# MoE down weights as four neighbouring rows per partition, gate and up columns dealt two of every four

## The reference

```
D_MODEL = 1024; SEQ = 512; DEPTH = 2; N_EXPERTS = 16; TOP_K = 2; D_EXPERT = D_MODEL // 2
...
    def expert_block(args):
        xblk, e = args
        h = jax.nn.silu(xblk @ w_gate[e]) * (xblk @ w_up[e])
        return h @ w_down[e]
```

## Time and profile before

| | before |
|---|---|
| time, median of 3 runs | 1109.61 us (1108.69 to 1113.83) |
| time of the profiled execution | 1114.09 us |
| its span in the trace | 1112.4 us |
| granted TensorE clock, mean | 0.939 of full speed |
| TensorE matmul busy | 968.1 us (87%) |
| weight issues: gate, up, down | 32 of each, 2048 KB each |
| HBM read, written | 250.33 MB, 53.74 MB |

### The profile page before, as it was taken

One profiled execution on the slowest core, in us unless ns is written; L12 is line 12 of the kernel. 1 busy time (PEld: TensorE's weight loads), 2 busy tenths in 40 slices (PEclk: granted clock), 3 DMA queues, 4 the chain that ended last, 5 costly groups with the idle time before them and its releaser, 6 DMA issues.

```text
span 1112.4 us, 15368 instructions
## 1 busy us (share of the span) xinstructions
PE 968.1 (87%) x5930; PEld 521.7 (47%) x5930; DVE 446.7 (40%) x909; ACT 163.9 (15%) x384; POOL 185.9 (17%) x304
## 2 busy tenths in 40 slices
PE   7999989999996879987669899968997969898994
PEld 4444344567553434543434454534664534454541
DVE  4799953551110111110675556575411212121116
ACT  0000022301110001000222332433010000010100
POOL 1320020213202022200430001011221210303022
PEclk9999989889998999999779999987998989999997
DMA  9994399946999999999730004200699999999953
GB/s 301 383 410 152 86 342 372 405 165 234 384 385 384 422 372 394 392 407 402 246 148 1 1 1 148 79 1 4 255 371 359 387 382 425 379 412 376 410 209 113
DMA packets 74614, 308.69 MB, mean 277 GB/s; under 512 B 9423, under 2 KB 21627, under 8 KB 58010
## 3 DMA queue, kind: packets, MB, share of 16 engines
q1 hardware_dynamic: 35744, 227.43, 53.2%
q10 hardware_dynamic: 28794, 54.03, 13.1%
q0 software_dynamic: 9984, 25.97, 6.7%
HBM read 250.33 MB, written 53.74 MB: 273 GB/s over the span
## 4 chain that ended last, share of the span: by engine, by line
PE 43%; DMA 21%; issue 17%; DVE 13%; POOL 2%; ACT 1%; ACTq 1%; SPq 1%; POOLq 0%; DVEq 0%
PE ps L724 15%; DMA wring<-in_moe_w_up_dram 9%; DVE arena L1067 7%; PE ps L734 7%; PE ps L624 6%; DMA wring<-in_moe_w_gate_dram 5%; PE ps L683 3%; PE ps L744 3%; DMA arena<-xs_dram 2%; PE ps L923 2%; PE ps L754 1%; DMA wring<-in_conv_w_dram 1%; POOL rstd L1841 1%; SPq L438 1%; PE ps L521 1%
## 5 line engine op out<-in xcount | busy, mean ns | idle before, releaser
L724 PE MATMUL ps<-wring,arena 128*64 128x256 f32 x1536 | 186.4, 398 | 23.3 <-DMA wring<-in_moe_w_gate_dram 16.8
L724 PEld LDWEIGHTS ps<-wring,arena 128*64 128x64 f32 x1536 | 114.2, 143 | 90.0 <-DMA wring<-in_moe_w_gate_dram 20.6
L560 PE MATMUL ps<-arena,wring 128*128 128x512 f32 x256 | 110.4, 593 | 1.4 <-DVE arena L1025 1.4
L1271 DVE COPY arena<-ps 128x256 f32<-128x256 f32 x32 | 13.6, 425 | 221.9 <-PE ps L832 211.2
L1067 DVE SCALAR_TENSOR_TENSOR arena<-arena,dwT 128x512 f32<-128x512 f32 x145 | 100.0, 764 | 0.0
L1855 POOL DMA_DIRECT2D arena<-xs_dram x112 | 59.5, 538 | 206.4 <-DVE arena L1250 164.0
L902 PE MATMUL ps<-wring,arena 128*128 128x512 f32 x192 | 86.5, 606 | 3.5 <-ACT arena L1697 3.5
L734 PE MATMUL ps<-wring,arena 128*64 128x512 f32 x384 | 86.5, 592 | 0.6 <-DVE arena L1271 0.6
L560 PEld LDWEIGHTS ps<-arena,wring 128*128 128x128 f32 x256 | 48.5, 190 | 62.1 <-issue 60.3
L724 PE MATMUL ps<-arena 128*64 128x256 f32 x512 | 63.4, 404 | 13.0 <-DMA arena<-in_moe_w_gate_dram 6.9
L1841 POOL TENSOR_TENSOR rstd<-vareps,half 128x1 f32<-128x1 f32 x20 | 24.7, 1235 | 294.9 <-DVE vareps L1084 294.9
(11 more groups left out here) (231 smaller groups left out, 1078.1 us busy)
## 6 DMA issues: line engine op xcount, KB each, us to landing
wring<-in_moe_w_gate_dram SPq DMA_DIRECT2D x24, 2048.0 KB, 23.6
wring<-in_moe_w_up_dram SPq DMA_DIRECT2D x24, 2048.0 KB, 20.0
wring<-in_moe_w_down_dram SPq DMA_DIRECT2D x24, 2048.0 KB, 19.7
xs_dram<-zero ACTq DMA_DIRECT2D x2, 16384.0 KB, 50.5
arena<-in_moe_w_up_dram SPq DMA_DIRECT2D x8, 2048.0 KB, 23.3
arena<-in_moe_w_down_dram SPq DMA_DIRECT2D x8, 2048.0 KB, 25.8
arena<-in_moe_w_gate_dram SPq DMA_DIRECT2D x8, 2048.0 KB, 28.9
xs_dram<-arena ACTq DMA_DIRECT2D x60, 128.0 KB, 8.8
```

Of the source, the lines that this page charges most:

```text
L560: last = pe.matmul(ps[:, 2 * (c % 4) + h, :], w[:, k, h, (c % 2) * P:(c % 2) * P + P], xT[:, k, :], start=(k == 0), stop=(k == KD - 1))
L724: mm = pe.matmul(ps[h * CAP:(h + 1) * CAP, bank, 0:256], act[:, k, :], w[:, k, h * 256:(h + 1) * 256], start=(k == 0), stop=(k == KD - 1))
```

## The change

Down is now loaded as `(p j)`: partition p takes the four neighbouring rows 4p to 4p+3, one run of 16 KB. For the products to come out in that order, the column groups of gate and up are dealt otherwise: group h takes, of every four neighbouring columns, the two at 2h and 2h+1. The 256 columns of one matmul, which were 256 neighbours, are now 128 pairs (8 bytes) with gaps of 8 bytes between them. Where a result stands is as before, so `stage_h`, `down_products` and `quarter_down` keep their code. No instruction is added, removed or moved on any engine; the down load changes its shape (from 128x2x2048 to 128x4096), and the gate and up matmuls the pattern by which they read the weights.

```diff
-        down_src = moe_w_down.rearrange("l e (h p j) n -> p (l e) h (j n)", h=2, p=P)
+        down_src = moe_w_down.rearrange("l e (p j) n -> p (l e) (j n)", p=P)
...
-                    sp.dma_start(slots[r].rearrange("p (h n) -> p h n", h=2), down_src[:, E * l + e, :, :]
-                                 ).then_inc(s_ring[r], 16)
+                    sp.dma_start(slots[r], down_src[:, E * l + e, :]).then_inc(s_ring[r], 16)
...
+            def columns(w, k, h):
+
+                return w[:, k, :].rearrange("p (i j) -> p i j", j=4)[:, :, 2 * h:2 * h + 2]
+
             def half_products(bank, act, w, signal, first=None):
 
                 for k in range(KD):
                     for h in range(2):
                         mm = pe.matmul(ps[h * CAP:(h + 1) * CAP, bank, 0:256], act[:, k, :],
-                                       w[:, k, h * 256:(h + 1) * 256], start=(k == 0), stop=(k == KD - 1))
+                                       columns(w, k, h), start=(k == 0), stop=(k == KD - 1))
...
                         mm = pe.matmul(ps[q * XROWS:(q + 1) * XROWS, bank, 0:256], xgxT[:, k, :],
-                                       gate_up[i][:, k, h * 256:(h + 1) * 256], start=(k == 0), stop=(k == KD - 1))
+                                       columns(gate_up[i], k, h), start=(k == 0), stop=(k == KD - 1))
```

## The result

The changed kernel is slower by 0.7%: 1123.1 us median of 20 runs (1113.5 to 1129.29) against 1115.41 us median of 20 runs of before (1107.56 to 1132.61); ratio 1.0071, 95% interval 1.0048 to 1.0093. The three runs of before that were known at first had a median of 1109.61 us, so the absolute forecast of 1109 us stood on a low draw; what counts is the ratio, and it is about 8 us. The forecast was no measurable change. The 1123.1 us lie inside its range of 1103 to 1133 us, but in the part that was there for rival 1.

A forecast was written before the change was run, and what follows sets the result against it. TensorE and the DMA engines were both taken as nearly full. The profiled 1114.1 us, minus 1 us for transfers, plus 0 for products, gave 1113 us; less 4.5 us to the median, about 1109 us, range 1103 to 1133 us.

The forecast's parts named there:

- rival 1: Gate, up and quarter products: each jump dear, product up to 3.89 us; likely +8 us (+3 to +22), chance 0.18.
- The transfers: Down loads on SP's queue: fewer, longer runs gain between 0 and 3.3 us, put down as 1 us.
- the products' reading: Gate and up weights streamed in pairs with gaps: likeliest cost nothing, up to 22 us by L683's dearest reading.
- The point from which it decides: Gate and up products: from 0.25 us more each, 22 products on the path pass 5.5 us.
- Rivals 2 and 3: 2: each streamed element dear, +290 us, chance 0.14; 3: down transfers gain more, 13 us off, chance 0.10.

The follow-up runs named there:

- down4_l1: Kernel before, with down loads of layer 1 alone in four runs of 4 KB; ratio 1.0023 (1.0000 to 1.0047).
- pairs_l1: Kernel before, with gate and up read in pairs of columns in layer 1 alone, down loads in 8 KB runs; ratio 1.0026 (1.0001 to 1.0052).
- pairs_8k: Changed kernel in both layers, but each down load goes as two runs of 8 KB; ratio to before 1.0073 (1.0042 to 1.0104).
- both_again: Changed kernel run again without edit, against the kernel before; ratio 1.0069 (1.0041 to 1.0097).
- every_other: Changed kernel, but each column group takes every second column in both layers; ratio to before 1.0070 (1.0038 to 1.0102).

## Why the prediction was wrong

**The transfers** were as forecast. A down load gained some 0.06 us where 0 to 0.10 us was put, the packets fell to 31648, and long down runs in layer 1 came out at 1.0013 with an interval that holds 1. The gain that was put down for them, 1 us, is below what any of these runs can tell.

**The step that failed** is the size of one term: "I take nothing for the likeliest value", for the products' reading. It measured 0.17 us a product, 11 ns a pass. The working held the right mechanism as its rival 1: L683 reads one element in each 32 bytes at 1.90 ns an element, and a pass of pairs needs 1.76 ns or less for each jump to keep its pace. The measured value, 1.84 ns, lies between the two, and the margin, of which the text said "missing is 8% at worst", was missing by 5%. The row was set aside on the grounds that it might be due to a load hidden badly; the runs with other patterns put nearly the same price, 1.79 to 1.84 ns, on the streamed operand. Whether L683 is slow for the same reason no run tested, and the row that was held against the price stands: the transposes of L521 read one element in each 32 bytes at 111 ns for 128, 0.87 ns each. So the price holds for the streamed operand of these matmuls, and not for every read that TensorE makes. The rival counted by jumps, and the runs show that 16-byte pieces are what counts; for pairs both counts are 128, and so its price was nearly right (0.29 against 0.17 us).

**The page of the Trainium skill** that the prediction weighed ("SBUF — State Buffer", section Specifications (TRN2)) says that two elements used of a line of 16 bytes are enough for full bandwidth. The unit is right: the runs follow pieces of 16 bytes. The threshold is a little too kind for a float32 stream: two used elements of four give 236 instead of 225 ns, four of eight give 225 ns, and one of four gives 459 ns.

**The point from which it decides** was set too high as well. Rival 1 was said to pass 5.5 us only from 0.25 us a product on, with 22 products on the path and layer 0 hiding all but 1 us. At 0.17 us a product this would have been 4 us, within 0.5%. Measured are about 8 us for 13 us of extra work. That rival 1 had put down +8 us as its likely value is luck: its price was too high and its share of the path too low, and the two cancel. Where the share was wrong is not settled. Layer 1 may give the 4 us or more (4.8 us in one set of runs, 2.9 us in the other), and layer 0 from nothing to 4.7 us, the end of its interval. The profiles put 0.8 of the 5.6 us of layer 1 ahead of the first gather on the chain (near 945 us) and 4.8 us behind it, where 14 products and 4 quarter products at 0.17 us make 3.1 us. Two of the six have the 3 us of the slow last down product there, which is 1 us of the mean, and the second gather on the chain lasted 0.9 us longer in the mean. The prediction also had this stretch all on TensorE, which it was not: in the kernel before, the chain crosses two gathers there, 8.62 us at 944.99 and 7.08 us at 1003.83.

**Rivals 2 and 3** fell: a dear element (7.8 us a product) happens only where each element lies in a piece of its own (7.34 us), the two column groups may read the same places at once without it (3.77 us), and no gain of the transfers showed.

## What to carry to other kernels

For a float32 operand that is streamed through the array, count the 16-byte pieces that a pass moves to, and multiply by 1.8 ns (measured at a granted clock of 1.00): if this is more than the pass takes now, expect it to set the pace. With 256 columns in two column groups, four neighbouring elements that fill a piece were free even with gaps between them, two in a piece cost 5%, and one in a piece doubled the pass. And before a layout is traded for longer transfer runs, read the service time of one transfer in a quiet stretch: here 8 KB runs were already as fast as 16 KB runs, so there was nothing to buy.

## What the runs showed of the hardware

- Runs of 8 KB and of 16 KB are served alike (4.9 to 5.0 us for 2 MB in a quiet stretch). But longer runs on one queue make small transfers on another land later: 64 KB gathers took 7.3 us at the median with the down loads of layer 1 in 4 KB runs (`down4_l1`), 7.6 to 7.7 us with all in 8 KB (`before`, `pairs_l1`, `pairs_8k`), and 8.7 to 8.8 us with all in 16 KB (`after`, `both_again`, `every_other`).
- Streams do not share the price of the pieces: a quarter product with four streams at once goes from 227 to 238 ns a pass, a product with two from 225 to 236 ns.
- Two profiles of one program can differ more than the change does: 1122.9 us and 1115.5 us for the changed kernel, of which about 3 us come from one late copy before the last product and the lower clock after it. What made that copy late was not found.
